# Gate matrices of an expert layer: three bf16 products from one-hots with tokens innermost in place of one fp32 product

## What is computed

```python
def peer_ffn(xn, w_query, sub_keys, u, v):
    def one_block(xb):                       # 128 tokens
        q = (xb @ w_query).reshape(BLOCK, PEER_HEADS, 2, PEER_HALF)
        s = jnp.einsum('thcd,hckd->thck', q, sub_keys)
        s1, i1 = lax.top_k(s[:, :, 0], PEER_TOPK)
        s2, i2 = lax.top_k(s[:, :, 1], PEER_TOPK)
        cand_s = (s1[..., :, None] + s2[..., None, :]).reshape(BLOCK, PEER_HEADS, PEER_TOPK * PEER_TOPK)
        cand_i = (i1[..., :, None] * N_KEYS + i2[..., None, :]).reshape(BLOCK, PEER_HEADS, PEER_TOPK * PEER_TOPK)
        top_s, top_c = lax.top_k(cand_s, PEER_TOPK)
        expert = jnp.take_along_axis(cand_i, top_c, axis=-1)
        g = jax.nn.softmax(top_s.astype(jnp.float32), axis=-1).astype(xb.dtype)
        ue = jnp.take(u, expert, axis=0)
        ve = jnp.take(v, expert, axis=0)
        act = jax.nn.gelu(jnp.einsum('thkd,td->thk', ue, xb), approximate=False)
        return jnp.einsum('thk,thkd->td', g * act, ve)
```

## Time and profile before

| | us |
|---|---|
| median of 3 runs | 1807.6 (1806.0 to 1811.88) |
| the profiled execution | 1812.57 |
| its span, first to last instruction | 1810.8 |
| PE busy | 1729.3 |
| DVE busy | 1345.6 |
| ACT busy | 724.2 |
| POOL busy | 665.5 |

### The profile page before, as it was taken

How to read it: one execution, slowest core, us unless ns; L and a number is a source line. 1 busy time by engine, 2 the same in 40 slices (tenths; PEclk the granted TensorE clock), 3 DMA queues, 4 the chain that set the end, 5 groups by cost and what they waited for, 6 DMA issues and landing times.

```text
span 1810.8 us, 25050 instructions
## 1 busy us (share of the span) xinstructions
PE 1729.3 (96%) x8891; PEld 1458.3 (81%) x8895; DVE 1345.6 (74%) x2716; ACT 724.2 (40%) x1162; POOL 665.5 (37%) x419
## 2 busy tenths in 40 slices
PE   7989998889898999999999999999999999999999
PEld 6767887555555779999999999999788888888887
DVE  5474855656655779899999913983788888888886
ACT  4333335231323234456345534553343444443332
POOL 4143330000000334777777776777322222222220
PEclk9999998999998999999999999999999999999999
DMA  4122213525344554598988898998999989999993
GB/s 159 42 93 70 93 47 117 186 94 186 138 141 140 183 164 145 185 335 295 349 296 295 296 354 309 334 310 289 393 353 324 338 325 336 326 337 328 331 337 123
DMA packets 170192, 429.78 MB, mean 237 GB/s; under 512 B 15328, under 2 KB 66144, under 8 KB 165744
## 3 DMA queue, kind: packets, MB, share of 16 engines
q1 hardware_dynamic: 133056, 294.23, 47.0%
q0 software_dynamic: 36864, 134.23, 20.5%
q10 hardware_dynamic: 176, 0.07, 0.0%
HBM read 384.44 MB, written 44.04 MB: 237 GB/s over the span
## 4 chain that ended last, share of the span: by engine, by line
PE 62%; DVE 15%; ACT 2%; DMA 2%; issue 2%; DVEq 0%; SPq 0%; POOL 0%; ACTq 0%
PE psum L1978 28%; PE psum L1170 6%; PE psum L1242 5%; PE psum L1240 5%; PE psum L1241 5%; PE psum L1266 3%; PE psum L1157 3%; DVE hot L1781 2%; PE psum L1070 2%; DVE rows_sb L1671 2%; DVE hits L1704 1%; DVE hot L1784 1%; DVE hits L1701 1%; DMA v<-in_v 1%; PE psum L1104 1%
## 5 line engine op out<-in xcount | busy, mean ns | idle before, releaser
L1486 POOL TENSOR_TENSOR ul<-u,uh 128x1024 fp32r<-128x1024 f32 x128 | 322.7, 2525 | 460.4 <-ACT uh L1400 458.6
L1240 PE MATMUL psum<-split,uh 128*128 128x384 f32 x1024 | 354.2, 346 | 3.2 <-POOL ul L1486 3.1
L1242 PE MATMUL psum<-split,ul 128*128 128x384 f32 x1024 | 343.3, 335 | 0.0
L1241 PE MATMUL psum<-split,uh 128*128 128x384 f32 x1024 | 342.6, 335 | 0.0
L1958 POOL DMA_INDIRECT v_row<-in_v,gv x128 | 123.5, 965 | 377.2 <-DVE psum L2044 368.5
L1978 PE MATMUL psum<-vl,wh 128*128 128x512 f32 x768 | 239.9, 393 | 0.0
L1240 PEld LDWEIGHTS psum<-split,uh 128*128 128x128 f32 x1024 | 192.7, 188 | 6.2 <-POOL ul L1486 4.5
L1241 PEld LDWEIGHTS psum<-split,uh 128*128 128x128 f32 x1024 | 192.7, 188 | 1.4 <-issue 1.4
L1242 PEld LDWEIGHTS psum<-split,ul 128*128 128x128 f32 x1024 | 192.2, 188 | 0.0
L1978 PEld LDWEIGHTS psum<-vl,wh 128*128 128x128 f32 x768 | 144.1, 188 | 33.7
L1781 DVE TENSOR_TENSOR hot<-iota,psum 128x1024 f32<-128x1024 f32 x96 | 116.8, 1217 | 65.0 <-PE psum L1254 57.2
(11 more groups left out here) (308 smaller groups left out, 3248.8 us busy)
## 6 DMA issues: line engine op xcount, KB each, us to landing
u<-in_u SPq DMA_DIRECT2D x128, 512.0 KB
v<-in_v SPq DMA_DIRECT2D x64, 1024.0 KB
act_mat<-act_w SPq DMA_DIRECT2D x128, 192.0 KB
act_v<-act_mat SPq DMA_DIRECT2D x64, 384.0 KB
wraw<-in_w_wide SPq DMA_DIRECT2D x18, 1024.0 KB, 5.3
gate_mat<-stage SPq DMA_DIRECT2D x16, 1024.0 KB
gate<-gate_mat SPq DMA_DIRECT2D x128, 128.0 KB
w_low<-in_w_branch_b SPq DMA_DIRECT2D x8, 1024.0 KB, 5.3
```

Source lines behind the costliest of these rows:

```text
L1240: nc.tensor.matmul(out, high[:, c], split[:, 0:DENSE, 0, c], start=(c == 0), stop=False)
L1241: nc.tensor.matmul(out, high[:, c], split[:, 0:DENSE, 1, c], start=False, stop=False)
L1242: last = nc.tensor.matmul(out, low[:, c], split[:, 0:DENSE, 0, c], start=False, stop=(c == DC - 1))
L1486: nc.gpsimd.tensor_tensor(ul[:, n % U_COLS], u[:, n % U_COLS], uh[:, n % UH_COLS].bitcast(F32), ALU.subtract).then_inc(s["u_low"], 1)
```

## The change

Everything that goes into the gate products becomes bfloat16.

- `settle` writes both indices as bf16 (whole numbers below 128) and splits the fp32 weight into three bf16 parts: a copy to bf16, a subtraction of it from the rest, and again (GATE_PARTS = 3). This adds three copies and two subtractions of 128x128 to `settle` for tiles 0 to 2.
- `turn_picks` transposes five bf16 arrays in place of three fp32 ones, into bf16 in PSUM.
- A copy of `iota` spread over four tokens (`iota_hot`, 128x512 bf16) is made once, ahead of `one_hot(1)`, after a wait for `s_out`.
- `hot` now has the keys ahead of the tokens: [P, 2, 4, N_KEYS, HOT], slot 0 the one-hot of the row index, slot 3 that of the column index. The comparison writes slots 0 and 3 (1024 elements), the multiplication writes slots 1 to 3 as slot 3 times the three parts (1536 elements). All operands are bf16; those from `turned` lie in PSUM.
- PE runs three bf16 products for each token, one per part, accumulated in PSUM: 12 for a group. Both operands are read at a step of four elements.

```diff
-    picks = high("picks", [P, 2, 3, PICKS])
+    picks = high("picks", [P, 2, 2 + GATE_PARTS, PICKS], BF16)
+    rest = high("rest", [P, PICKS])
...
-    hot = placer(nc, m.gates_at + GATHERED * 2 * ROW, m.stage_at)("hot", [P, 2, 2, HOT, N_KEYS])
+    hot = placer(nc, m.gates_at + GATHERED * 2 * ROW, m.stage_at)("hot", [P, 2, 1 + GATE_PARTS, N_KEYS, HOT], BF16)
+    iota_hot = placer(nc, m.keysT_at + 3 * ROW // 4, m.spare_at)("iota_hot", [P, N_KEYS, HOT], BF16)
...
-                for k in range(3):
-                    last = nc.tensor.transpose(bank(m, 2)[:, k * P:(k + 1) * P], picks[:, (i - 1) % 2, k], m.ident[:])
+                turned = bank(m, 2).bitcast(BF16)
+                for k in range(2 + GATE_PARTS):
+                    last = nc.tensor.transpose(turned[:, k * P:(k + 1) * P], picks[:, (i - 1) % 2, k], m.ident_b[:])
...
-                        last_mm = nc.tensor.matmul(bank(m, 6 + b)[:, q * P:(q + 1) * P], hot[:, b, 0, q],
-                                                   hot[:, b, 1, q], start=True, stop=True, skip_group_check=True)
+                        for p in range(GATE_PARTS):
+                            last_mm = nc.tensor.matmul(bank(m, 6 + b)[:, q * P:(q + 1) * P], hot[:, b, 0, :, q],
+                                                       hot[:, b, 1 + p, :, q], start=(p == 0), stop=(p == GATE_PARTS - 1),
+                                                       skip_group_check=True)
...
-                    weight = picks[:, tile % 2, 2]
+                    weight = rest[:]
...
+                for p in range(GATE_PARTS):
+                    part = nc.vector.tensor_copy(picks[:, tile % 2, 2 + p], rest[:])
+                    if p < GATE_PARTS - 1:
+                        link(part)
+                        link(nc.vector.tensor_tensor(rest[:], rest[:], picks[:, tile % 2, 2 + p], ALU.subtract))
+                part.then_inc(s["picks_ready"], 1)
...
-                    keys = bcast(bcast(m.iota[:], 1, HOT), 1, 2)
-                    nc.vector.tensor_tensor(hot[:, b], keys, bcast(turned[:, 0:2, some], 3, N_KEYS), ALU.is_equal
-                                            ).then_inc(s["hot_rows"], 1)
+                    nc.vector.tensor_tensor(hot[:, b, 0::GATE_PARTS], bcast(iota_hot[:], 1, 2),
+                                            bcast(turned[:, 0:2, some], 2, N_KEYS), ALU.is_equal).then_inc(s["hot_rows"], 1)
                     dve.wait_ge(s["hot_rows"], n + 1)
-                    nc.vector.tensor_tensor(hot[:, b, 0], hot[:, b, 0], bcast(turned[:, 2, some], 2, N_KEYS), ALU.mult
-                                            ).then_inc(s["hot_ready"], 1)
+                    nc.vector.tensor_tensor(hot[:, b, 1:], bcast(hot[:, b, GATE_PARTS], 1, GATE_PARTS),
+                                            bcast(turned[:, 2:, some], 2, N_KEYS), ALU.mult).then_inc(s["hot_ready"], 1)
...
             chosen(2)
+            dve.wait_ge(s["s_out"], 2 * NT)
+            link(nc.vector.tensor_copy(iota_hot[:], bcast(m.iota[:], 2, HOT)))
             one_hot(1)
```

More of the change, by code:

```diff
@@ L830 @@
 HIT_HEADS = 2
+GATE_PARTS = 3
 STORED = DENSE - 1
@@ L1730, in settle @@
                                                bcast(norm[:], 2, PEER_TOPK), ALU.mult)
+                link(last)
                 if tile == GATHERED:
-                    link(last)
-                else:
-                    last.then_inc(s["picks_ready"], 1)
+                    return
+                for p in range(GATE_PARTS):
[4 more added lines that the diff above has]
+                part.then_inc(s["picks_ready"], 1)
             def chosen(r, i=0):
@@ L1773, in one_hot @@
                 dve.wait_ge(s["picks_turned"], i)
-                turned = bank(m, 2)[:, 0:3 * P].rearrange("p (a t) -> p a t", a=3)
+                turned = bank(m, 2).bitcast(BF16)[:, 0:(2 + GATE_PARTS) * P].rearrange("p (a t) -> p a t", t=P)
                 for g in range(TURNS * TURN_GROUPS):
```

## The result

The changed kernel takes 1860.07 us (median of 4 runs) against 1807.88 us (median of 4), a ratio of 1.0278 (95% interval 1.0257 to 1.030): 52 us slower, where 19 us faster was forecast. The profiled execution has a span of 1860.3 us.

The account below looks back on a forecast made before the run. PE and DVE were both taken to bound a group: 2.995 us falling to 2.79, 0.20 less x 96 = 19.2 us, so 1807.6 - 19.2 = 1788.4 us; range 1781 to 1822, likeliest case 1781 to 1796.

Parts of the forecast that it names:

- What bounds the kernel: In the gate turns of the three dense tiles, PE and DVE are saturated at once, 2.995 us a group, 96 groups.
- The gate products: On PE, twelve bf16 products at 0.057 us take 0.68 in place of 0.90 a group; PE's group becomes 2.77.
- my upper bound of 0.112: Slowest time allowed for a bf16 gate product on PE: today's fp32 record, as if the step halved the rate.
- rival 2: The strided step slows PE's gate products to 0.112 us each: group 3.43, +42 us, 1850; chance 0.06.
- The point from which it decides: From 0.075 us a gate product, PE is no faster than before the change.
- Load and product taking turns: In PE's run of twelve, 0.085 us a product: group 3.11, +11 us, 1819; chance 0.08.
- The one-hots on DVE: Comparison and multiplication run at double rate, 0.72 and 0.865 us; with the dot product at 1.14, DVE's group is 2.73.
- The joint of a group: PE at 2.77 and DVE at 2.73, tied across two buffers, get 0.02 us extra: 2.79 a group.
- DMA and the other engines: They keep up in the turns: ACT busy 3.75 of 5.58 us a column, DMA share 0.955, near but not binding.
- the floor of 2.75 a group: DMA's limit on the column work: 5.5 us a column, so a group cannot go below 2.75 us.
- The small parts: `iota_hot`, additions to `settle`, bf16 transposes, tail: net 0; `settle` adds 1.4 us before turn two, offset by DVE's lead.
- My upper bound of +2.5: Largest net loss in us allowed for `settle` of tile 2 before turn two, where PE waits; lower bound -1.

Follow-up runs that it names:

- e8: The changed kernel with keys innermost in `hot`, so PE reads adjacent elements and DVE reads a token's value at a step of zero: 1910.39 us.
- e6: The changed kernel with the moving operand of the gate products read at a step of three elements, weights at four: 1829.39 us.
- e4: The changed kernel with both operands of the gate products read at a step of two elements in place of four: 1798.98 us.
- e1: The changed kernel with both operands of the gate products read as 128 adjacent elements: 1791.88 us.
- e5: The changed kernel with `hot` laid out in pairs of tokens innermost, so PE reads both operands at a step of two: 1794.24 us.
- e3: The changed kernel with the weights of the gate products read adjacent and only the moving data at a step of four: 1855.5 us.
- e7: The changed kernel with the moving operand of the gate products read at a step of eight elements, weights at four: 2029.48 us.
- e10: The kernel before the change, with the moving operand of its fp32 gate products read at a step of four elements: 1889.78 us.
- e2: The changed kernel with the moving operand of the gate products read adjacent and only the weights at a step of four: 1796.27 us.

## Why the prediction was wrong, point by point

**What bounds the kernel: right.** PE and DVE both limited a group. A kernel with DVE at 2.73 and PE slower gained nothing from DVE, and e8, with PE faster, gained nothing from PE.

**The gate products: wrong, and this is the step that failed.** I took 0.057 us from a contiguous row and wrote "since nothing in the trace reads an operand slower than another of its type". That was no evidence: no operand of PE in the trace was read at a step at all. The measured 0.117 lies just above my upper bound of 0.112, and rival 2 (1850, chance 0.06) named the mechanism and came within 10 us. That it is a doubling was taken from the fp32 record without a reason ("as if the step halved the rate"), so its size is a lucky guess; its chance and the range were wrong. The point from which it decides (0.075) fits: e6 at 0.091 is slower than before, e4 at 0.059 faster. The rule that I set beside this step, a stride up to eight bf16 at full rate (the Trainium skill, SBUF — State Buffer, "Door 1: The DMA port swizzle"), is contradicted here for moving data: three elements cost 1.6 times, four 2.1 times, eight 4.1 times. For weights at a step of four it nearly agrees (0.058).

**Load and product taking turns: did not happen.** Twelve in a row go at 0.056. The Trainium skill's 81 ns for sustained pairs (TensorE: Matmul & The Clock Gate, "Back-to-back issue gap") is not borne out by e1.

**The one-hots on DVE: right in each number.** 0.72 for the comparison and 0.865 for the multiplication, start to start, were forecast; 0.72 and 0.87 are in the rows (802.33, 803.05, 803.92). The rule that spoke against the change, single rate with any PSUM operand (the Trainium skill, VectorE: DVE Perf Modes, "The perf-mode tier table"), does not hold for these two instructions; the 0.52 ns an element of the Trainium skill, PSUM — Partial Sum Buffer, "Specifications (TRN2)", does. And e8 shows the other half: a step of zero innermost takes the rate away.

**The joint of a group: 0.04 too small.** With adjacent reads the group is 2.83, not 2.79. In e1 the twelve products and the way back to the columns take 0.74 (2.83 less 2.09), where 12 x 0.056 is 0.67. The 0.07 lies nearly all in the way back. The first weight load of the run starts 0.16 us late behind those of the columns, but its product starts 0.18 after the one before it (801.95 to 802.13), about a column step, so that costs next to nothing. From the start of the last gate record to the second column product it is 0.29 us in both kernels: 803.76 - 802.69 less seven steps of 0.112 before, 803.04 - 802.13 less eleven of 0.056 in e1. My sum has one product and one column product there, 0.057 + 0.174 = 0.23; with an fp32 record of 0.112 the same sum gives 0.29, which hid it. It is worth 4 us over 96 groups.

**DMA and the other engines: right.** e1 and e5 run at shares of 0.93 to 0.96 in the turns, and PE waits for the low part of `u` 0.3 and 0.8 us in all; the floor of 2.75 a group was not reached.

**The small parts: right.** The five new operations in `settle` took 1.4 us ahead of turn two, and the weight's product was blocked as in rows 8 (2.07 us, 1.81 before). PE waited 1.33 us there against 0.97. My upper bound of +2.5 is not too wide: in e3 and e4 a later operation of `settle` was the one held up, and PE waited 2.60 and 3.56 us. The changed kernel's rows:

```profile
954.40 2.07 DVE L1735 TENSOR_TENSOR rest<-top,norm 128x128 f32<-128x128 f32 x1
956.51 0.23 DVE L1741 CAST picks<-rest 128x128 bf16<-128x128 f32 x1
...
957.83 0.68 DVE L1791 TENSOR_TENSOR hot<-iota_hot,psum 128x1024 bf16<-128x1024 bf16 x1
...
959.56 1.58 PE L1271 MATMUL psum<-hot 128*128 128x128 bf16 x12 [1.33 <-DVE hot L1794]
```

So with the products at their contiguous rate the sum would have held: 1788.4 forecast, 1791.9 (e1) and 1794.2 (e5) measured.

## What to carry to other kernels

A layout change serves two readers. Price it for each: here tokens innermost halved DVE's time an element and doubled PE's time a product, and only the slower of the two counts. Where one end of an unknown cost has no row behind it, a missing row is no reason to take the cheap end. If DVE needs adjacent pairs, give it pairs and no more: a step of two elements was free for PE's moving data, four was not.

## What the runs showed of the hardware

Moving data of a 128-column product, in us, by the distance from one element to the next:

| bytes | bf16 product | fp32 record |
|---|---|---|
| 2 | 0.056 (step 1) | |
| 4 | 0.059 (step 2) | 0.112 (step 1) |
| 6 | 0.091 (step 3) | |
| 8 | 0.117 (step 4) | 0.114 (step 2) |
| 16 | 0.229 (step 8) | 0.224 (step 4) |

In each type a step of two elements is free and four double the time. Whether elements or bytes set it is open, since both fit. Weights at a step of four made a group 0.04 us longer and a product 0.002.

The granted clock can fall in a turn although PE counts as busy. In e7 it stood at 0.57 behind a run at a step of eight. Slow reads alone do not do it: e10, whose fp32 records are as slow (0.224), kept 1.00 over the whole of turn one (763 to 865 us). In neither did PE wait. e7 has twelve such records in a row and e10 eight, and the type differs; which of these matters was not tried. In the changed kernel, at turn two, after PE's wait of 1.33 us and one run at a step of four:

```profile
958.00:961.00 3.00, 1.67 (x15) 1.42 (x14) 2.96 (x5) 0.00 (x0) 0.08 (x1) 1.00 0.48 184
961.00:964.00 3.00, 3.00 (x12) 3.00 (x11) 2.94 (x5) 1.07 (x1) 1.22 (x2) 0.53 0.47 120
```

It was back at 1.00 by 967 us; eleven column products took 3.48 us in place of 1.91, so it cost about 1.6 us. The other runs say a little on what tips it. Waits of 1.30 to 1.52 us in that place with faster moving reads (e1, e2, e5, e6) were followed by no fall, and a wait of 3.56 us with products of 0.059 (e4) was followed by 0.52. So the fall in e4 needed no slow read, while behind a wait as short as the changed kernel's only the run at a step of four was followed by a fall. That is one execution of each kernel, and no proof.
